# A recurrent mixer's features and first running product on GpSimd, its PSUM evacuations merged or split by bank

## The reference, cut to what matters

```python
def step(s, inp):
    r_t, w_t, k_t, v_t, kk_t, a_t = inp
    s = (s * w_t[:, :, None, :]
         - jnp.einsum('bhij,bhj->bhi', s, kk_t)[..., None] * (kk_t * a_t)[:, :, None, :]
         + v_t[..., None] * k_t[:, :, None, :])
    return s, jnp.einsum('bhij,bhj->bhi', s, r_t)

decay = jnp.exp(-jnp.exp(w_log))
a = jax.nn.sigmoid(lp['rwkv_a0'] + jnp.einsum('btdr,drc->btdc', ad, lp['rwkv_a_up']))
k_dir = heads(k[:, :, None, :] * (1.0 + (a - 1.0) * lp['rwkv_k_a']))
```

## Time and profile before

| | us |
|---|---|
| median of 3 runs | 3335.96 |
| lowest and highest run | 3335.18 and 3340.79 |
| span of the profiled execution | 3341.8 |

### The profile page before, as it was taken

How to read it: one execution, slowest core, us unless ns; L and a number is a source line. 1 busy time by engine, 2 the same in 40 slices (tenths; PEclk the granted TensorE clock), 3 DMA queues, 4 the chain that set the end, 5 groups by cost and what they waited for, 6 DMA issues and landing times.

```text
span 3341.8 us, 62748 instructions
## 1 busy us (share of the span) xinstructions
PE 3229.7 (97%) x25596; PEld 3036.0 (91%) x25596; DVE 2441.0 (73%) x4488; ACT 1296.1 (39%) x2435; POOL 86.1 (3%) x116
## 2 busy tenths in 40 slices
PE   8999999999988999999999999999999889999998
PEld 7999999888776999999989999998877669999997
DVE  6877777654879577677887877776458876776766
ACT  5333334222445443333543343342134634333333
POOL 0001100000000000000001000000000000000000
PEclk9999999999999999999999999999999989999999
DMA  3222223221042222222222312232300521122221
GB/s 111 70 84 77 88 70 120 74 100 66 4 153 108 76 64 70 66 75 65 75 70 81 94 57 84 82 117 70 120 24 22 199 80 50 61 71 76 67 76 70
DMA packets 89262, 266.27 MB, mean 80 GB/s; under 512 B 10152, under 2 KB 18472, under 8 KB 87696
## 3 DMA queue, kind: packets, MB, share of 16 engines
q1 hardware_dynamic: 84656, 248.35, 22.6%
q0 software_dynamic: 4320, 13.91, 1.4%
HBM read 232.33 MB, written 29.88 MB: 78 GB/s over the span
## 4 chain that ended last, share of the span: by engine, by line
PE 87%; DVE 8%; issue 2%; ACT 1%; DMA 1%; SPq 0%; POOL 0%; DVEq 0%; ACTq 0%
PE ps L1031 51%; PE ps L1111 36%; DMA wring<-wa 1%; DVE wl L2417 1%; PE ps L1607 0%; DVE sc L3070 0%; DMA x<-xT 0%; DVE uv L3022 0%; DVE gl L2611 0%; DVE x L2320 0%; DVE M2X L2793 0%; ACT sqb L1718 0%; DVE sc L3081 0%; DVE olocal L2919 0%; DVE Mrk L2780 0%
## 5 line engine op out<-in xcount | busy, mean ns | idle before, releaser
L1111 PE MATMUL ps<-gh,wh 128*128 128x384 f32 x2488 | 839.1, 337 | 24.2 <-DVE gl L2616 13.7
L1111 PE MATMUL ps<-gh,wl 128*128 128x384 f32 x2488 | 834.5, 335 | 0.0
L1111 PE MATMUL ps<-gl,wh 128*128 128x384 f32 x2488 | 834.5, 335 | 0.0
L1111 PEld LDWEIGHTS ps<-gh,wh 128*128 128x128 f32 x2488 | 468.9, 188 | 33.1 <-issue 10.5
L1031 PE MATMUL ps<-act_high,wh 128*128 128x384 f32 x1408 | 478.4, 340 | 2.0 <-DVE act_low L2483 2.0
L1031 PE MATMUL ps<-act_high,wl 128*128 128x384 f32 x1408 | 471.9, 335 | 0.0
L1031 PE MATMUL ps<-act_low,wh 128*128 128x384 f32 x1408 | 471.8, 335 | 0.0
L1111 PEld LDWEIGHTS ps<-gl,wh 128*128 128x128 f32 x2488 | 469.2, 189 | 0.5
L1111 PEld LDWEIGHTS ps<-gh,wl 128*128 128x128 f32 x2488 | 469.1, 189 | 0.0
L2320 DVE SCALAR_TENSOR_TENSOR x<-ps,x 128x384 f32<-128x384 f32 x416 | 227.1, 554 | 225.1 <-PE ps L1031 224.6
L1739 ACT CAST wh<-wring 128x512 fp32r<-128x512 f32 (+2 forms) x260 | 183.2, 706 | 466.3 <-PE ps L1031 389.7
(11 more groups left out here) (306 smaller groups left out, 4973.0 us busy)
## 6 DMA issues: line engine op xcount, KB each, us to landing
wring<-wa SPq DMA_DIRECT2D x244, 512.0 KB, 3.5
wring<-wa SPq DMA_DIRECT2D x128, 256.0 KB, 2.6
wring<-wa SPq DMA_DIRECT2D x64, 192.0 KB, 2.3
bias<-bias SPq DMA_DIRECT2D x24, 512.0 KB, 7.6
conv_q_k<-stage SPq DMA_DIRECT2D x28, 384.0 KB, 2.5
kern_rows<-kst POOLq DMA_DIRECT2D x24, 256.0 KB, 3.4
outT<-x SPq DMA_DIRECT2D x2, 3072.0 KB, 9.7
kern<-kern_rows SPq DMA_DIRECT2D x12, 512.0 KB, 7.2
```

The source lines that it names most:

```text
L1111: m = pe.matmul(out, lhs[a], rhs[b], start=start and n == 0, stop=stop and n == 2, skip_group_check=onto)
```

## The change

1. GpSimd makes the eight elementwise feature steps of each pass (`features`) and `X = sq_a + eye` of each group. The scan, the difference and the small copy into `pc` stay on VectorE. The decay's scale moves into the exponentials, the scan one place ahead, and the order of the four small rate products changes, so that the rates `a` come first.
2. Tiles are laid beside each other (`AB`, `CK`, `QM`) and masks so that one strided slice of constants serves several targets. VectorE then takes stages 0 and 1 with one 128x768 instruction a group, and stage 2 with one 128x256 and one 128x512.
3. Stages 7 and 8 are split by bank: VectorE copies the first bank of a group, ScalarE the second. VectorE adds the identity of stage 7 behind both.

```diff
-        PREPARE_AT = {(4, 1): "decay", (5, 0): "scan", (5, 1): "cum", (5, 2): "rate", (6, 0): "key", (6, 1): "ksum", (6, 2): "keys",
-                      (7, 0): "alpha", (7, 2): "feat_ab", (8, 0): "rho", (8, 2): "feat"}
+        PREPARE_AT = {(4, 1): "scan", (5, 0): "cum", (7, 2): "ends"}
...
+            def features(l, q):
+
+                d, i = divmod(q, 2)
+                F, rates, M = feat[q % 2], kap[:, :, :].rearrange("p c t -> p (c t)"), ALU.mult
+                in_chunks = lambda t: t.rearrange("p (c t) -> p c t", t=CH)
+                pool.wait_ge(*ra_.at(l, "sig", q, 3 if q == 0 else 1))
+                pool.tensor_scalar(rates, tmp[:, 1, :], prm("rwkv_k_a", i), dpar[:, 16 + i:17 + i], M, ALU.add)\
+                    .then_inc(*rg.inc(l, "rate", q))
+                pool.wait_ge(*rg.at(l, "rate", q))
+                pool.tensor_tensor(rates, rates, pa[:, 2 + i, :], M).then_inc(*rg.inc(l, "key", q))
+                pool.wait_ge(*rg.at(l, "key", q))
+                if q < 2:
+                    pool.tensor_copy(ksum[:, i, :], rates).then_inc(*rg.inc(l, "ksum", q))
+                else:
+                    pool.tensor_tensor(ksum[:, i, :], ksum[:, i, :], rates, ALU.add).then_inc(*rg.inc(l, "ksum", q))
+                if q == 0:
+                    pool.wait_ge(*rv.at(l, "kk", 1))
+                pool.tensor_tensor(F[:, :, BETA, :], in_chunks(kk[:, i, :]), in_chunks(tmp[:, 1, :]), M)\
+                    .then_inc(*rg.inc(l, "keys", q))
+                pool.wait_ge(*ra_.at(l, "expE", q))
+                pool.tensor_tensor(F[:, :, ALPHA, :], in_chunks(kk[:, i, :]), in_chunks(tmp[:, 0, :]), M)\
+                    .then_inc(*rg.inc(l, "alpha", q))
+                pool.wait_ge(*rg.at(l, "keys", q))
+                pool.wait_ge(*ra_.at(l, "expN", q))
+                pool.tensor_tensor(F[:, :, BETA, :], F[:, :, BETA, :], in_chunks(tmp[:, 2, :]), M)\
+                    .then_inc(*rg.inc(l, "feat_ab", q))
+                pool.tensor_tensor(F[:, :, RHO, :], in_chunks(pa[:, i, :]), in_chunks(tmp[:, 3, :]), M)\
+                    .then_inc(*rg.inc(l, "rho", q))
+                pool.tensor_tensor(kap[:, :, :], kap[:, :, :], in_chunks(tmp[:, 2, :]), M).then_inc(*rg.inc(l, "feat", q))
...
+                features(l, 0)
+                for q in range(4):
+                    for g in range(GROUPS):
+                        h = slice(4 * g, 4 * g + 4)
+                        pool.wait_ge(*rv.at(l, "b", q, 0, g))
+                        pool.tensor_tensor(QM[:, h, X, :], AB[:, h, SQ, :], eye_b(4), ALU.add)\
+                            .then_inc(*rg.inc(l, "one", q, g))
+                    if q < 3:
+                        pool.wait_ge(*rp.at(l, "b", q, 1, GROUPS - 1))
+                        features(l, q + 1)
...
                 elif s == 7:
-                    sa.copy(outer(sq_b[:, h, :]), quad(o, 256, 192)).then_inc(*ra_.inc(l, "turned", q, g))
-                    sa.copy(outer(sq_a[:, h, :]), quad(o, 256, 0))
-                    m = sa.copy(outer(Q[:, h, :, :].rearrange("p c a t -> p c (a t)")), quad(o, 256, 64, 128))
+                    m = sa.copy(of_chunks(QM, g, 1), ps[:, o + 1, :].rearrange("p (j w) -> p j w", j=2))
                 elif s == 8:
-                    sa.copy(inner(sq_c[:, h, :]), quad(o, 192, 0))
-                    m = sa.copy(inner(NR[:, h, 1:3, :].rearrange("p v a t -> p v (a t)")), quad(o, 192, 64, 128))
+                    sa.copy(CK[:, 4 * g + 2:4 * g + 4, SQ, :], of_head(o + 1, 0, 1))
+                    m = sa.copy(NR[:, 4 * g + 2:4 * g + 4, 0:2, :].rearrange("p v a t -> p v (a t)"), of_head(o + 1, 1, 2))
...
                 if s == 0:
-                    TT(inner(sq_a[:, h, :]), quad(o, 192, 0), mask_in(up[0]), M)
-                    TT(inner(btok_Mrb[:, h, 1, :]), quad(o, 192, 64), mask_in(up[3]), M)
-                    m = ve.tensor_copy(inner(btok_Mrb[:, h, 0, :]), quad(o, 192, 128))
+                    m = TT(AB[:, h, :, :], slots(o, 0, 3), masks_in(*BLOCK_MASKS[d]), M)
...
                 elif s == 2:
-                    TT(inner(sq_b[:, h, :]), quad(o, 128, 64), mask_in(low[0]), M)
-                    TT(inner(NR[:, h, 0, :]), quad(o, 128, 64), mask_in(low[1]), M)
-                    TS(inner(NR[:, h, 1, :]), quad(o, 128, 0), -1.0, None, M)
-                    m = TT(X, sq_a[:, h, :], eye_b(4), AD)
+                    TT(sq_b[:, h, :].unsqueeze(2), slots(o, 1, 1), masks_in((LOW_D, UP_D)[d], 1, 1), M)
+                    m = TT(NR[:, h, 1:3, :], slots(o, 0, 2), masks_in(*OFF_MASKS[d]), M)
...
                 elif s == 7:
-                    m = TT(NR[:, h, 0, :], sq_b[:, h, :], eye_b(4), AD)
+                    step(ve.tensor_copy(of_chunks(QM, g, 0), ps[:, o, :].rearrange("p (j w) -> p j w", j=2)))
+                    ve.wait_ge(*ra_.at(*k, s, g))
+                    m = TT(NR[:, h, OFF, :], QM[:, h, X, :], eye_b(4), AD)
+                elif s == 8:
+                    ve.tensor_copy(CK[:, 4 * g:4 * g + 2, SQ, :], of_head(o, 0, 1))
+                    m = ve.tensor_copy(NR[:, 4 * g:4 * g + 2, 0:2, :].rearrange("p v a t -> p v (a t)"), of_head(o, 1, 2))
```

More of the change, by code:

```diff
@@ L446, in k_rv @@
                 out += [("ksq", i), ("kmax", i), ("vt", i), ("kk", i)]
-            out += [("cum", 0), ("keys", 0), ("feat_ab", 0), ("feat", 0)]
+            out += [("cum", 0), ("ends", 0)]
             for q in range(4):
@@ L460, in k_rv @@
                             out += [("bonus", s - 4)]
-                        if q < 3 and PREPARE_AT.get((s, g)) in ("cum", "keys", "feat_ab", "feat"):
+                        if q < 3 and PREPARE_AT.get((s, g)) in ("cum", "ends"):
                             out += [(PREPARE_AT[s, g], q + 1)]
@@ L473, in build, with k_rg @@
         FILTER_JOBS = [FILTER_AT[u] for u in sorted(FILTER_AT)]
+        def k_rg():
+            made = lambda q: [(n, q) for n in ("rate", "key", "ksum", "keys", "alpha", "feat_ab", "rho", "feat")]
+            return made(0) + [e for q in range(4) for e in [("one", q, g) for g in range(GROUPS)] + (made(q + 1) if q < 3 else [])]
         def k_fp():
@@ L586, in units, with masks_in, slots @@
             return ps[:, b, 0:HALF].rearrange("p (c t) -> p c t", t=CH)
-        def mask_in(m):
-            o = COFF["masks"] + CH * m
-            return cst[:, o:o + CH].unsqueeze(1).unsqueeze(1).broadcast_to([P, 2, 2, CH])
+        def masks_in(first, step, n):
+            at = COFF["masks_before"]
+            row = cst[:, at:at + 11 * CH].rearrange("p (m t) -> p m t", t=CH)
+            end = first + n * step
+            return row[:, first:end if end >= 0 else None:step, :].unsqueeze(1).broadcast_to([P, 4, n, CH])
+        def slots(b, a, n):
+            return ps[:, b:b + 2, :].rearrange("p b (j w) -> p (b j) w", w=256)[:, :, CH * a:CH * a + CH * n]\
+                .rearrange("p v (a t) -> p v a t", t=CH)
         def quad(b, width, a, n=CH):
@@ L1271, in batch @@
                     pe.wait_ge(*ra_.at(l, "b", q - 1, BATCH - 1, g))
+                sq_a, sq_c = part(AB, SQ), part(CK, SQ)
+                if s == 4:
+                    pe.wait_ge(*rg.at(l, "one", q, g))
                 if s == 0:
-                    m = into_pairs(g, 192, 0, 192, part(F, BETA), parts(F, ALPHA, 3))
+                    m = into_pairs(g, 192, 0, 256, part(F, BETA), parts(F, ALPHA, 3))
                 elif s == 1:
-                    m = into_pairs(g, 192, 0, 192, one(kap), parts(F, ALPHA, 3))
+                    m = into_pairs(g, 192, 0, 256, one(kap), parts(F, ALPHA, 3))
@@ L2810, in prepare @@
             def prepare(l, q, part):
-                d, i = divmod(q, 2)
-                F, kf = feat[q % 2], flat(kap[:, :, :])
-                if part == "decay":
+                if part == "scan":
                     ve.wait_ge(*ra_.at(l, "sig", q, 3))
-                    step(TS(tmp[:, 0, :], tmp[:, 0, :], DECAY_SCALE, None, M))
-                elif part == "scan":
                     if q < 2:
@@ L3151, in _ @@
                     scale_qk(l, i)
-                    for part in {1: ("decay", "scan", "cum"), 2: ("rate", "key", "ksum", "keys"), 3: ("alpha", "feat_ab"),
-                                 4: ("rho", "feat")}.get(i, ()):
+                    for part in {1: ("scan", "cum"), 4: ("ends",)}.get(i, ()):
                         prepare(l, 0, part)
```

159 lines of the change are left out of this document (71 added, 88 removed).

## The result

Measured side by side, five rounds each: 3351.69 us (3351.58 to 3354.58) against 3338.29 us (3335.18 to 3340.85) for the kernel before. The ratio is 1.0038, 95% interval 1.0025 to 1.0051: **slower by 13.4 us**. The profiled execution of the change took 3353.38 us, span 3351.5 us, 9.7 us above the span before.

A forecast was written before the change was run, and what follows sets the result against it. TensorE, busy 97%, was taken as the bound, so only its waits in the mixer could be won. Six passes losing 1.85 us (11.1) less 0.8 won in fourth passes gave 3335.96 + 10.3 = 3346 us, range 3322 to 3355.

The forecast's parts named there:

- Stages 0 to 2, 0.8 us won: Merged VectorE evacuations cut a pass's work from 10.0 to 8.0 us, so PE starts stage 3 at 849.8, not 850.61.
- The rival that they are not cheaper: Stages 0 to 2: a 128x768 evacuation holds VectorE 1.0 us like its three parts; 3352 us, chance 0.07.
- Stages 3 to 6: With fewer features on VectorE, stage 6 starts at 862.0, stage 7 at 863.6, and the first exponential ends at 864.7.
- P, the POOL addition: Length of one 128x768 feature on GpSimd beside stage 7: taken as 1.9 us, from 1.69 to 2.21, break-even 1.44.
- The rival with the speed of copies: GpSimd's features run as fast as its copies, P 1.25 to 1.45 us: 3331 to 3335 us, chance 0.10.
- The meeting: Stage 7's three VectorE additions each wait for a GpSimd feature, both with two SBUF inputs, ending at 868.85, 871.0, 873.1.
- The start of stage 9: In layer 0's second pass PE starts stage 9 at 873.8 instead of 871.96, 1.85 us lost a pass.
- Stages 9 and 10 ... stay: These stages have no VectorE instruction with two SBUF inputs, so their times were taken as unchanged.
- Issue: 1.1 us of PE's waits in layer 0's second pass, for which no other engine is to blame.
- Sum: Six passes with features lose 1.85 us each, 11.1 us; the fourth passes win 0.8 us for two; together +10.3 us.
- `pc` at 0.1 us and the early features at nothing: The copy into `pc` behind stage 7's additions takes 0.1 us; GpSimd's early features, from the end of stage 1, cost nothing.
- the 1 us that it set aside: Third passes: cost if stage 3 fails to cover early features meeting the small state additions; counted in the range's upper end.

The follow-up runs named there:

- experiments 1 to 3: The changed kernel with stage 7's addition reading one operand from PSUM (3331.92 us), GpSimd's late features waiting for the additions (3329.45 us), or those features in halves (3338.64 us).
- experiment 3: The changed kernel with each of GpSimd's four late features as two instructions over half the columns: 3338.64 us, ratio 0.9988 to the kernel before.
- experiments 1, 8 and 9: The changed kernel with stage 7's addition from PSUM: alone (3331.92 us), with X back on VectorE (3339.63 us), with ScalarE's table load ahead of stage 5's copies (3324.51 us).
- experiment 6: The kernel before with only the eight features moved to GpSimd, masks, evacuations and X as before: 3360.32 us, ratio 1.0061 to the kernel before.

## Why the prediction was right, point by point

Forecast 3346 us (3322 to 3355), slower; measured 3351.7. Times of the after trace are given here less 2.81 us, the difference between the two traces at the first small rate product of the pass (841.99 and 844.80).

- **Stages 0 to 2, 0.8 us won: right.** The 128x768 evacuations from two banks last 0.95 us (the row L2837 above), and stage 3 starts at 849.65 (forecast 849.8). The rival that they are not cheaper is out; that its 3352 us is what was measured is chance.
- **Stages 3 to 6: right.** Stage 6 at 861.75 (862.0), stage 7 at 863.18 (863.6), the first exponential ends at 864.49 (864.7).
- **P, the POOL addition: right, 0.08 high.** 1.81 to 1.83 us undisturbed where 1.9 was taken (the estimate from the Trainium skill, GPSIMD Engine Reference, Elementwise — side-by-side cycle accounting, was 1.81), 2.0 when a DVE addition takes its turn. The rival with the speed of copies is out.
- **The meeting: right**, by rows and by experiments 1 to 3. The additions end at 868.45, 870.4 and 872.35, forecast 868.85, 871.0 and 873.1.
- **The start of stage 9: right for the wrong reason.** Forecast 873.8, measured 873.74. But DVE was ready 0.8 us sooner; PE's third group of stage 8 ran at half clock and took 1.34 us instead of 0.68. Stage 9 then took 3.57 from its start to stage 10's, instead of 2.42 in the kernel before: another 1.15 us which no term of the sum held. "Stages 9 and 10 ... stay" is the sentence that failed: the prediction has the wait, but not TensorE's clock behind it.
- **Issue.** Against that the pause at this pass's start, 1.1 us in the earlier trace rows, is 0.2 now. So it isn't a fixed price; what makes it was not tried.
- **Sum.** A pass costs 2.1 us more in passes 1 and 2 of layer 0, 3.4 and 2.0 in layer 1, and -0.4 and +1.8 in the third passes: 11.1 us over six (1.85 each, as forecast), and the fourth passes win 1.0 (0.8). That this agrees is partly luck: the clock's loss, the smaller P, the shrunken pause and a third pass without loss in layer 0 cancel. In third passes products of the read and the chain of states fill part of PE's wait, which is 2.3 us for the additions there. The clock over the third pass is 0.96 in both kernels in layer 0, but in layer 1 it is 1.00 before and 0.96 now, and there the third pass does lose.
- **The time.** Of the 5.7 us above the forecast, 2.3 are the base: before measured 3338.3 beside the change, not 3336.0. The medians then differ by 13.4 us, the profiled spans by 9.7; the passes explain the latter. The 3.7 us between the two were not traced: the execution of the kernel before that was profiled has a span of 3341.8 us, longer than the time of any of its five runs.
- **`pc` at 0.1 us and the early features at nothing.** For `pc` this is true in the change itself, where the late additions had pushed it behind GpSimd's last feature (0.16 us); with the additions mended, it is followed by 0.7 us of PE's wait. The early features do meet something, in stage 2 of the third passes. There a small state addition with two SBUF inputs, 0.29 us alone, takes 1.90 us, and PE waits 0.45 us for the evacuation behind it:

```profile
895.49 1.90 DVE L2929 TENSOR_TENSOR state<-state,inject 128x128 f32<-128x128 f32 x1
```

The prediction saw this meeting and took stage 3 as cover; the wait stands ahead of it, within the 1 us that it set aside.

## What to carry to other kernels

Before work goes to GpSimd, list the VectorE instructions that will run beside it and count their SBUF inputs: those with two, and SBUF to SBUF copies even of 12 columns, may each wait for one whole GpSimd instruction. Read one operand from PSUM, let the long instruction start later, or move the exposed one too; which engine had less work said nothing here. And a wait of TensorE in a stage where it is thinly busy anyway can have a second price, the clock behind it: look at the granted clock of the stretch, not at the waits alone.

## What the runs showed of the hardware

- PE busy 1.6 us out of 4, at 868 to 872, is followed by a granted clock near 0.5 for about 6 us (872 to 878), 0.77 in the next 2. In experiment 3 the longest single wait was 1.7 us instead of 2.4; behind it the clock stayed at 1.00 in the second pass of layer 0 and was 0.5 for 3.4 us in that of layer 1. It also fell for 3.4 us behind pauses at a pass's start alone (before, at 882.2, behind 1.4 us).
- A VectorE copy of 12 columns from SBUF to SBUF takes 0.16 to 0.17 us alone and 1.17 to 1.36 beside a GpSimd feature of 128x768 (experiments 1, 8 and 9). A 128x256 addition with two SBUF inputs takes 0.42 alone and up to 2.06 (experiment 6), a 128x128 one 0.29 and 1.90. With one operand in PSUM the 128x256 addition takes 0.41 to 0.43 in either case.
- GpSimd's side of a meeting is 0.2 us: 2.0 for 1.82. Halving its instructions cut VectorE's longest addition from 1.78 to 1.11 us.
